# Gate and up of two experts' steps in three products of rounded parts, in a kernel of five blocks on one core

## The reference

```python
hg = jnp.einsum('cd,edf->cef', xc, w_eg)      # gate, D 1024 -> FF 256
hu = jnp.einsum('cd,edf->cef', xc, w_eu)      # up
a = jax.nn.silu(hg) * hu * gch[..., None]
return jnp.einsum('cef,efd->cd', a, w_ed)     # down, FF 256 -> D 1024
```

## Time and profile before

| | us |
|---|---|
| median of 3 runs | 1326.91 (1326.29 to 1327.44) |
| the profiled execution | 1327.36 |
| its span in the trace | 1325.6 |
| start of the first gather | 942.3 |
| start of the first step 0 | 948.6 |
| end of the last step's down | 1316.3 |
| PE busy | 1229.8 |
| DVE busy | 709.4 |
| ACT busy | 476.3 |

### The profile page before, as it was taken

How to read it: one execution, slowest core, us unless ns; L and a number is a source line. 1 busy time by engine, 2 the same in 40 slices (tenths; PEclk the granted TensorE clock), 3 DMA queues, 4 the chain that set the end, 5 groups by cost and what they waited for, 6 DMA issues and landing times. The chain is left out here.

```text
span 1325.6 us, 18074 instructions
## 1 busy us (share of the span) xinstructions
PE 1229.8 (93%) x6940; PEld 906.3 (68%) x6940; DVE 709.4 (54%) x1467; ACT 476.3 (36%) x835; POOL 99.7 (8%) x131
## 2 busy tenths in 40 slices
PE   5998998999889988999788999998899999999997
PEld 5888777798677967798677687885544544544453
DVE  4666677573776557664468887766222222122223
ACT  4242464442744445443653434631111221221120
POOL 1031000600014000000110210000000000000000
PEclk9989898999989999999999999899899999999999
DMA  9452472554815562544505453031799988988870
GB/s 352 155 195 103 147 263 81 203 183 161 316 65 190 205 241 84 185 163 171 116 2 197 160 191 128 9 127 32 300 421 412 381 328 303 372 356 305 325 297 32
DMA packets 99253, 273.58 MB, mean 206 GB/s; under 512 B 14961, under 2 KB 20337, under 8 KB 83441
## 3 DMA queue, kind: packets, MB, share of 16 engines
q1 hardware_dynamic: 96160, 268.52, 55.5%
q10 hardware_dynamic: 3026, 4.14, 0.9%
HBM read 271.60 MB, written 1.05 MB: 206 GB/s over the span
## 5 line engine op out<-in xcount | busy, mean ns | idle before, releaser
L1453 ACT ACTIVATE weights_high<-ring 128x2048 fp32r<-128x2048 f32 (+2 forms) x88 | 160.2, 1869 | 196.0 <-PE psum L720 68.1
L1893 DVE TENSOR_TENSOR weights_low<-ring,weights_high 128x2048 fp32r<-128x2048 f32 (+2 forms) x88 | 194.4, 2242 | 29.8 <-ACT weights_high L1453 28.9
L1242 PE MATMUL psum<-expert,gathered 128*32 128x512 f32 (+1 forms) x768 | 174.1, 595 | 0.0
L720 PE MATMUL psum<-input_high,weights_high 128*128 128x256 f32 x480 | 137.8, 287 | 4.7 <-DVEq L1924 4.0
L720 PE MATMUL psum<-input_high,weights_low 128*128 128x256 f32 x480 | 137.3, 286 | 0.0
L720 PE MATMUL psum<-input_low,weights_high 128*128 128x256 f32 x480 | 137.2, 286 | 0.0
L1242 PEld LDWEIGHTS psum<-expert,gathered 128*32 128x32 f32 (+1 forms) x768 | 62.3, 136 | 85.1 <-issue 84.5
L732 PE MATMUL psum<-weights_high,input_high 128*128 128x512 f32 (+2 forms) x272 | 102.6, 377 | 2.4 <-issue 1.9
L732 PE MATMUL psum<-weights_high,input_low 128*128 128x512 f32 (+2 forms) x272 | 101.3, 372 | 0.0
L732 PE MATMUL psum<-weights_low,input_high 128*128 128x512 f32 (+2 forms) x272 | 101.1, 372 | 0.0
L720 PEld LDWEIGHTS psum<-input_high,weights_high 128*128 128x128 f32 x480 | 93.8, 195 | 5.4 <-DVEq L1924 4.4
(11 more groups left out here) (393 smaller groups left out, 2319.2 us busy)
## 6 DMA issues: line engine op xcount, KB each, us to landing
expert<-in_exp_gate_up SPq DMA_DIRECT2D x80, 1024.0 KB, 8.9
expert<-in_exp_down SPq DMA_DIRECT2D x40, 1024.0 KB, 12.1
ring<-in_w_ada SPq DMA_DIRECT2D x12, 2048.0 KB, 8.1
ring<-in_b_w_in SPq DMA_DIRECT2D x8, 2048.0 KB, 9.0
ring<-in_d_w_in SPq DMA_DIRECT2D x8, 2048.0 KB, 8.9
ring<-in_a_w_in SPq DMA_DIRECT2D x7, 2048.0 KB, 8.9
ring<-in_c_w_in SPq DMA_DIRECT2D x7, 2048.0 KB, 7.8
ring<-in_w_in SPq DMA_DIRECT2D x7, 2048.0 KB, 8.0
```

The source lines that it names most:

```text
L720: last = nc.tensor.matmul(bank[:, 256 * f:256 * f + 256], w2_[x][:, d, col + 128 * f:col + 128 * f + 128], in2[y][:, d, :], start=(k == 0) ...
L1242: last = nc.tensor.matmul(hid_bank[w * k:w * k + w, :], xg[:, d, 128 * j + w * k:128 * j + w * k + w], guv[i][:, d, :], start=(d == 0), st ...
L1453: nc.scalar.activation(hi_half(m, k), ring[i][:, x], ACT.Copy).then_inc(s_wh, 1)
L1893: v.tensor_tensor(w_lo[i][:, x], ring[i][:, x], hi_half(m, k), ALU.subtract).then_inc(s_wl, 1)
```

## The change

- Steps 0 and 1 take gate and up in three products per chunk (`PARTS`): high input x high weights, high input x low weights, low input x high weights. Step 2 and all down products stay native f32.
- `gathered` splits in three tiles. ACT copies 256 of the 384 columns rounded (`gathered_high`, the slots of steps 0 and 1) and the last 128 plain (`gathered_third`). DVE takes the rest of the 256 columns (`gathered_low`), after ACT.
- The weights of experts 0 and 1 are split on the chip, in two pieces of 2048 columns each. ACT rounds a piece into the one tile `expert_high`, which both experts use in turn; DVE subtracts it and writes the rest in place, over the loaded weights (`expert_low0`, `expert_low1`). Expert 1's pieces are made in step 0. Expert 0's, for the iteration to come, are made in step 2; for the first iteration ahead of its gather.
- PE waits for `expert_low_ready` in place of the loads, and for `gathered_low_ready` in place of `gathered_ready`. Gather's banks go 0, 1, 2, 3, 0, 1, 2, 3, so that from the fifth chunk on it waits for the chunk four before it, and for `y_low`'s two halves ahead of the third and fourth.
- The last iteration is written out behind the loop, which runs six times, so that it doesn't split weights for an iteration that isn't there. It doesn't build a next `Sel` either. `rounds` is a second register read from the list.
- Memory is laid out anew to make room: constants that are used early share theirs with `expert_high` and the activations, and are loaded in a transfer of their own; `expert_low` lies over experts 0 and 1.

```diff
+                if j < 2:
+                    for d in chunks:
+                        for n, (x, y) in enumerate(PARTS):
+                            last = nc.tensor.matmul(hid_bank[:, :], xg[x][:, d, 128 * j:128 * j + 128], (guh, gul)[y][j][:, d, :],
+                                                    start=(d == 0 and n == 0), stop=(d == DC - 1 and n == 2))
...
                 if j == 0:
-                    pe.wait_ge(s_xg, iteration * 8 + 3)
-                pe.wait_ge(gu_in[j][0], (iteration + 1) * (16 * len(LOADS[j])))
+                    pe.wait_ge(s_xl, iteration * 8 + 5)
+                if j < 2:
+                    pe.wait_ge(s_el, part + 1)
+                else:
+                    pe.wait_ge(gu_in[j][0], (iteration + 1) * (16 * len(LOADS[j])))
...
                 for k in range(DC):
-                    if k == 4 and not first:
-                        pe.wait_ge(s_yl, iteration * 6)
-                    if k in (2, 3, 6, 7):
-                        pe.wait_ge(s_xg, iteration * 8 + k - 1)
+                    if k == 2 and not first:
+                        pe.wait_ge(s_yl, before * 6 + 5)
+                    if k == 3 and not first:
+                        pe.wait_ge(s_yl, before * 6 + 6)
+                    if k >= 4:
+                        pe.wait_ge(s_xl, iteration * 8 + k - 3)
                     gather(k)
...
-                    nc.scalar.activation(xg[:, k, :], gather_bank[k][:, 0:3 * P], ACT.Copy).then_inc(s_xg, 1)
+                    nc.scalar.activation(xg[0][:, k, :], gather_bank[k][:, 0:2 * P], ACT.Copy)
+                    nc.scalar.activation(xgt[:, k, :], gather_bank[k][:, 2 * P:3 * P], ACT.Copy).then_inc(s_xg, 1)
+
+            def expert_high(j, p, iteration, before=None):
+
+
+                act.wait_ge(gu_in[j][p], (iteration + 1) * 16)
+                if before is not None:
+                    act.wait_ge(gu_free[p], before + 1)
+                nc.scalar.activation(eh_[:, PIECES[p]], experts[j][:, PIECES[p]], ACT.Copy).then_inc(s_eh, 1)
...
                 gathered(iteration)
-                for j in range(3):
-                    sigmoid(iteration * 3 + j)
-                    y_high(iteration * 3 + j)
-
+                g = iteration * 3
+                expert_high(1, 0, iteration, g)
+                sigmoid(g)
+                expert_high(1, 1, iteration, g)
+                y_high(g)
+                sigmoid(g + 1)
+                y_high(g + 1)
+                if not last:
+                    for p in range(2):
+                        expert_high(0, p, iteration + 1, g + 1)
+                sigmoid(g + 2)
+                y_high(g + 2)
...
+            def expert_low(j, p, iteration):
+
+                dve.wait_ge(s_eh, iteration * 4 + (2 * j + p + 1))
+                v.tensor_tensor(el_[j][:, PIECES[p]], experts[j][:, PIECES[p]], eh_[:, PIECES[p]], ALU.subtract).then_inc(s_el, 1)
+
+            def gathered_low(iteration):
+
+                for k in range(DC):
+                    dve.wait_ge(s_xg, iteration * 8 + k + 1)
+                    v.tensor_tensor(xg[1][:, k, :], gather_bank[k][:, 0:2 * P], xg[0][:, k, :], ALU.subtract).then_inc(s_xl, 1)
+
+            def items(iteration, last=False):
+
+                gathered_low(iteration)
+                g = iteration * 3
+                for j in range(2):
+                    select_T_in(g + j, j)
+                    activate(g + j)
+                    act_T_in(g + j)
+                    if j == 0:
+                        expert_low(1, 0, iteration)
+                        expert_low(1, 1, iteration)
+                    y_low(g + j)
+                select_T_in(g + 2, 2)
+                if not last:
+                    select(iteration + 1)
+                    expert_low(0, 0, iteration + 1)
+                    expert_low(0, 1, iteration + 1)
+                activate(g + 2)
+                act_T_in(g + 2)
+                y_low(g + 2)
+
+            for p in range(2):
+                expert_low(0, p, 0)
             items(0)
-            with dve.Fori(0, more) as it:
+            with dve.Fori(0, rounds) as it:
                 items(it + 1)
+            items(more, last=True)
```

More of the change, by code:

```diff
@@ L162, in build @@
         sb("over_probsT_end", P, 2048 - T * 3 * P - 3 * S - 280)
-        experts = [sb(f"expert{i}", P, SLOT + 2 * D) for i in range(ROLES)]
+        with ExitStack() as loaded:
+            experts = [sb(f"expert{i}", P, SLOT + 2 * D, stack=loaded) for i in range(2)]
+        with ExitStack() as lows:
+            el_ = []
+            for i in range(2):
+                el_.append(sb(f"expert_low{i}", P, SLOT, dt=f32r, stack=lows))
+                sb(f"over_down{i}", P, 2 * D, stack=lows)
+        sb("over_experts", P, 2 * SLOT + 4 * D)
+        experts += [sb(f"expert{i}", P, SLOT + 2 * D) for i in range(2, ROLES)]
+        xgt_ = sb("gathered_third", P, DC * P)
         h = h_[:, :].rearrange("p (t n) -> p t n", t=T)
@@ L280, in build @@
         hid_bank, misc, y_bank = banks[0], banks[1], banks[2:4]
-        gather_bank = [banks[i] for i in (0, 1, 0, 1, 2, 3, 2, 3)]
+        gather_bank = [banks[k % 4] for k in range(DC)]
         in2 = [x[:, :].rearrange("p (c s) -> p c s", s=S) for x in (uTh_, uTl_)]
@@ L1372, in _ @@
             items(0, first=True)
-            with pe.Fori(0, more) as it:
-                items(it + 1)
+            with pe.Fori(0, rounds) as it:
+                items(it + 1, it)
+            items(more, rounds)
             pe.wait_ge(s_yl, more * 6 + 6)
```

98 lines of the change are left out of this document (57 added, 41 removed).

## The result

The changed kernel takes **1319.57 us** (median of six runs, 1315.06 to 1322.45), the one before 1326.86 (six runs, 1326.26 to 1329.63). The ratio is 0.9937 [0.9917, 0.9957]: 7.3 us less, faster by more than the 2.7 us that can be told from no change. The time forecast was 1315.5, in a range of 1306 to 1323.

The account below looks back on a forecast made before the run. PE was taken as the bound, DMA next. Against the profiled 1327.36 us, -24.0 (products) - 1.6 (gather) + 9.5 (step 2) + 4.7 (first iteration) = -11.4; against the median 1315.5 us, range 1306 to 1323.

Parts of the forecast that it names:

- rival 1: As summed, with a stall in step 2 of 1.0 to 1.9 us, either product price: 1311 to 1319; chance 0.64.
- rival 3: Gather turns into ACT's pace, up to 0.8 us an iteration, 6 us in all: 1318 to 1323; chance 0.13.
- The bound: In a settled iteration PE is the bound and DMA the next one, with about a tenth to spare.
- The products: Gate_up of whole-array steps: three products of parts replace each native chunk, gaining 1.5 us a step, 24.0 us over 16.
- scatter's price: 0.2325 us a product where banks change, as in scatter: a gain of 1.4 us a step, 22.4 in all.
- Gather: Gather's waits for ACT at the third and seventh chunk go: 0.2 us an iteration, 1.6 in all.
- Expert 1's splits: Made in step 0 on ACT and DVE while PE works: free; uncovered they would cost 4.5 us a step.
- Step 2's stall: Expert 0's two pieces on DVE delay `activate`: 1.35 us of PE idle in seven iterations, +9.5 us.
- Rival 2: The stall in step 2 is not there, or half: 1306, up to 1311; chance 0.09.
- The first iteration: Unhidden splits delay gather's fifth chunk by 3.0 us, and low clock adds 1.7 once: +4.7 us.
- Rival 4: PE's idle time in step 2 lowers the granted clock: 1327.4, no change, or 1330, slower; chance 0.14, half slower.
- point of decision: For the case of a lowered clock in step 2: it decides from 1.65 us an iteration on.

Follow-up runs that it names:

- four products: The changed kernel with a fourth product per chunk, low input x low weights, in the sixteen whole-array steps: 1348.75 us, 1.0146 of before.
- native on high parts: The changed kernel with one native f32 product of the high parts per chunk in place of three, all splits kept: 1340.84 us, 1.0080 of before.
- stall and a half more: The changed kernel with one more DVE reduction over 1024 columns in step 2, behind the two subtractions: 1334.42 us, 1.0033 of before.
- gather first: The changed kernel with all gathered chunks ahead of expert 0's second piece in the first iteration: 1318.51 us, 0.9926 of before.
- GpSimd takes a piece: The changed kernel with expert 0's second piece behind act_T's copy, and subtracted by GpSimd in the first iteration: 1311.18 us, 0.9849 of before.
- piece after act_T: The changed kernel with DVE's rest of expert 0's second piece moved behind act_T's copy in step 2: 1309.74 us, second look 1310.68 us.

## Why the prediction was right

The time lies in the range, and the mechanism is rival 1's. By its number alone, 1319.57 lies 0.6 above that rival's own 1311 to 1319 and inside rival 3's 1318 to 1323, whose mechanism isn't there. So the terms decide, not the median.

**The bound.** PE was the bound and still is. Between the start of step 0 and step 2 no idle time came in, and what the products save there arrived in the period, in the experiments as in the changed kernel.

**The products: right in kind, too large in size.** -24.0 us was forecast, 1.5 a step; -21.0 was measured, 1.31. The difference of 0.19 has three parts in the rows after. The products start 0.231 us apart (sixteen distances between 1089.19 and 1092.89), which is nearer to scatter's 0.2325 than to the projection's 0.2275: 0.09 for 24. The two transposes for select_T take 0.18 and not the 0.12 that I took off the native chunks, so these were 6.92: 0.06. And behind one product, where the transposes end, the next start is 0.28 off in place of 0.23 (1088.91 to 1089.19): 0.05. I had given scatter's price as the bound, 22.4; the truth lies 1.4 beyond it. A fourth product cost 0.227, so the price taken was that of one more product; the mean over a step is a little above it. With four products a chunk the distances in the row are 0.230; why they are 0.231 with three, no run tells. For 512 columns the Trainium skill (TensorE: Matmul & The Clock Gate, Back-to-back issue gap) has two prices: 0.216 us, which it calls that of a single product and the prediction took for a row of them, and 0.131 for a stream with weight loads. The trace agrees with neither, as no distance in this stream is below 0.22.

**Gather.** -1.6 was forecast, -2.2 measured (8 x 0.28). Both breaks went: behind the first distance the rows of PE's gather are 0.176 apart throughout. ACT is not its pace; of its rows for one chunk, 0.39 and 0.27 us, the first has 0.15 idle ahead of it:

```profile
1083.30 0.39 ACT L1751 ACTIVATE gathered_high<-psum 128x256 fp32r<-128x256 f32 x1 [0.15 <-PE psum L1251]
1083.58 0.27 ACT L1752 ACTIVATE gathered_third<-psum 128x128 f32<-128x128 f32 x1
```

So rival 3 fell; the estimate of 0.28 for the 128 columns was right.

**Expert 1's splits are free**, as forecast: no wait of PE for `expert_low` stands in the loop's waits.

**Step 2's stall.** +9.5 us forecast, +7.6 measured: 1.09 an iteration and not 1.35. The two pieces took 4.48 us as forecast, and that was luck: the 2.24 of L1893 is the mean of several shapes (the row says "+2 forms"), not of 88 like ones. One of 2048 columns takes 2.28 here, and two of them overlap by 0.08. The pair starts at 1116.21, 0.07 before `select`'s last row ends, and the first instruction of `activate` starts 0.08 before the second piece ends. That is 0.15 of the 0.26. The rest is rounding of mine: 1121.35 + 4.48 is 1125.83, which is 1.25 behind the old start of 1124.58, and I had made 1.35 of it. The experiment behind act_T took the stall away, and the one with reductions made it in the kernel before. Rival 2, that it isn't there, fell.

**The first iteration.** +4.7 forecast. It was 48.49 us before and 51.04 after, 1.99 and 6.34 above the settled period: +4.35. The parts differ from those named: the hole is 3.39 and not 3.0, the low clock behind it costs 2.3 (sixteen products 0.32 apart and not 0.176), some 0.3 more pass at the two ends of the hole, and the 1.7 us that step 0's down had lost before were not lost this time. I had added one fall to the one that was there; in this profile, in the second one of the same kernel and in three others one took the place of the other. In "four products", "native on high parts" and "stall and a half more" both are there, and the first iteration is some 1.8 us longer for it. So that the term came out so near to 4.7 is in part luck.

**The clock.** Rival 4 was a real mechanism at the wrong length. Its point of decision, 1.65 us an iteration, was a time that the rival needed to win, and no claim on how long a wait must be. The runs give that: none of the waits of 1.04 to 1.08 us in five kernels lowers the clock, 1.86 does in "gather first" and 1.92 in "GpSimd takes a piece" does not, 2.2 does in five cases of seven, 3.25 in seven of seven. Step 0's 1.53 and 0.61 in the first iteration lowered it in six of the twelve profiles: in the kernel before, "gather first", "four products", "native on high parts", "GpSimd takes a piece" and "stall and a half more". In the other six, both of the changed kernel among them, they did not. By the Trainium skill (TensorE: Matmul & The Clock Gate, HAM oscillation) bursts with waits between them can pay for the clock in every round. The runs with the longer stall agree: five iterations of seven at 2.2 us, all seven at 3.25.

**The sum.** -21.0 - 2.2 + 7.6 + 4.35 = -11.3, against the -11.1 that the loop's time shows and the -11.4 of the prediction. The terms' errors, +3.0, -0.6, -1.9 and -0.35, cancel all but 0.1. So the total was better than its parts.

**The median.** It is 4.1 us above the forecast. In the two profiles of the changed kernel that isn't from any term, since the loop's time agrees with the sum to some 0.2 us in both. By these two, and the two of "piece after act_T", what differs from one execution to the next is ahead of the loop, by 2.2 and 5.9 us. That the other five executions behind the median differ there too is likely and not shown, since only one of the six was profiled; a second low stretch in the first iteration, as three kernels had it, would add 1.8 as well. I made the sum against a profile and three runs that lay within 1.2 us and took this for the spread; twelve runs of before spread over 9.5. The two comparisons give -7.3 and -9.6, against -11.1 in the loop. If the changed kernel draws more low clock in the attention layers than before, which it could by a different placing of the constants, no run here shows it. The two profiles with the old places (942.28 and 943.99 us to the first gather) lie in the midst of the ten with the new ones (939.48 to 948.92); that stays open.

## What to carry to other kernels

When work is moved to an idle engine, ask not how much it idles but what is queued behind the new instruction: 4.5 us of splits filled a 3.2 us idle time and took 7.6 us back, and one of the two pieces moved three lines down raised the gain in the loop from 11.1 to 18.5 us. Measure a part of a kernel between two marks of the trace, here from the first gather product to the end, when the rest of it spreads by more than the effect. And a wait of PE can have a second price in clock: here 1.07 us cost its length alone, and 2.2 us cost 1.4 to 1.7 more in five iterations of seven.

## What was not expected of the hardware

- A wait of 2.2 us lowered TensorE's clock in five cases of seven and not in two, in one execution of one kernel with the same instructions; the low stretch costs 1.4 to 1.7 us. One of 1.86 us did and one of 1.92 did not, in two kernels. Waits of 1.53 and 0.61 us, 0.4 us of work apart, did so in six profiles of twelve.
- Where the rows of products change from one kind to another and back, 0.05 us are lost though no wait is shown (0.28 in place of 0.23). Whether the change or a semaphore that was already there does it was not tried.
- GpSimd's subtraction of 128x2048 elements took 4.63 us, only twice DVE's 2.28.
- The attention layers, which the change doesn't touch, made 5.9 us of difference between two executions of one kernel, while its loop agreed to 0.3.
